# Layer norms of a two-layer decoder step: the first chunk behind a norm input tile by input tile, three tiles centered behind the reciprocal

## The reference

```python
def _layer_norm(x, g, b):
    xf = x.astype(jnp.float32)
    mu = jnp.mean(xf, axis=-1, keepdims=True)
    var = jnp.mean(jnp.square(xf - mu), axis=-1, keepdims=True)
    return ((xf - mu) * lax.rsqrt(var + LN_EPS) * g.astype(jnp.float32) + b.astype(jnp.float32)).astype(x.dtype)
...
        # per sub-layer: x = _layer_norm(DN_ALPHA * x + sublayer(x), g, b)
```

## Time and profile before

| | |
|---|---|
| median of 3 runs | 3062.95 us (3060.9 to 3064.45) |
| the profiled execution, its own time | 3062.5 us |
| its span in the trace | 3060.7 us |
| mean granted TensorE clock | 0.996 |
| busy: PE, DVE, ACT, POOL | 3016.8, 1985.3, 1628.1, 125.0 us |

### The profile page before, as it was taken

The page is one execution under the profiler, slowest core; times in us unless marked ns, Lnnn a source line. Parts: engine busy times, 40 slices in busy tenths (PEclk is TensorE's granted clock), DMA queues, the critical chain, the costliest instruction groups (busy, mean ns, idle before and its releaser), DMA issues.

```text
span 3060.7 us, 60293 instructions
## 1 busy us (share of the span) xinstructions
PE 3016.8 (99%) x25089; PEld 2948.4 (96%) x25089; DVE 1985.3 (65%) x2512; ACT 1628.1 (53%) x1744; POOL 125.0 (4%) x222
## 2 busy tenths in 40 slices
PE   9999999999999999999999999999999999999997
PEld 9999899999999999999999999999999999999997
DVE  5455454677655666667758888777686566556665
ACT  4435575545444445445556767775454444445453
POOL 1010100000000000000000111100000000000000
PEclk9999999999999999999999999999999999999998
DMA  7565667544445445544456776665444544455452
GB/s 273 183 239 205 225 218 278 193 159 167 165 180 199 169 178 205 191 164 179 179 218 216 240 243 230 235 210 194 179 162 179 196 175 172 182 202 182 178 192 84
DMA packets 94523, 598.07 MB, mean 195 GB/s; under 512 B 11120, under 2 KB 11136, under 8 KB 33312
## 3 DMA queue, kind: packets, MB, share of 16 engines
q1 hardware_dynamic: 68688, 498.17, 44.0%
q0 software_dynamic: 25680, 97.69, 9.2%
HBM read 558.66 MB, written 37.15 MB: 195 GB/s over the span
## 4 chain that ended last, share of the span: by engine, by line
PE 92%; DVE 5%; ACT 1%; issue 1%; DMA 1%; DVEq 0%; POOL 0%; POOLq 0%; SPq 0%; ACTq 0%
PE acc L653 29%; PE acc L654 28%; PE acc L655 28%; DVE lo L563 1%; PE aux L2103 1%; PE aux L2426 1%; PE aux L2459 1%; PE aux L2440 1%; DVE x L1789 1%; DVE xl L1802 1%; DVE x L1797 1%; ACT xh L1188 0%; ACT hi L553 0%; PE aux L2188 0%; DMA x<-xsave 0%
## 5 line engine op out<-in xcount | busy, mean ns | idle before, releaser
L653 PE MATMUL acc<-xh,hi 128*128 128x264 f32 x7552 | 2174.8, 288 | 10.0 <-DVE lo L563 5.0
L654 PE MATMUL acc<-xl,hi 128*128 128x264 f32 x7552 | 2146.5, 284 | 0.0
L655 PE MATMUL acc<-xh,lo 128*128 128x264 f32 x7552 | 2139.0, 283 | 0.0
L653 PEld LDWEIGHTS acc<-xh,hi 128*128 128x128 f32 x7552 | 1422.9, 188 | 26.6 <-issue 13.9
L654 PEld LDWEIGHTS acc<-xl,hi 128*128 128x128 f32 x7552 | 1423.1, 188 | 4.2
L655 PEld LDWEIGHTS acc<-xh,lo 128*128 128x128 f32 x7552 | 1419.9, 188 | 0.0
L563 DVE TENSOR_TENSOR lo<-raw,hi 128x2048 fp32r<-128x2048 f32 x473 | 1077.7, 2287 | 381.2 <-ACT hi L553 380.5
L553 ACT ACTIVATE hi<-raw 128x2048 fp32r<-128x2048 f32 x473 | 897.6, 1907 | 492.6 <-DMA raw<-in_w 324.0
L552 ACT ACTIVATE xh<-pj 128x1056 fp32r<-128x1056 f32 x144 | 156.0, 1083 | 340.2 <-PE acc L655 279.6
L560 DVE TENSOR_TENSOR xl<-pj,xh 128x1056 fp32r<-128x1056 f32 x144 | 180.7, 1255 | 203.5 <-ACT hi L553 200.2
L1512 DVE SCALAR_TENSOR_TENSOR stage<-acc,par,stage 128x255 f32<-128x255 f32 x352 | 168.9, 480 | 23.1 <-DVE stage L1512 21.9
(11 more groups left out here) (284 smaller groups left out, 1609.3 us busy)
## 6 DMA issues: line engine op xcount, KB each, us to landing
raw<-in_w SPq DMA_DIRECT2D x473, 1024.0 KB, 4.9
x<-in_ssm POOLq DMA_DIRECT2D x32, 512.0 KB, 4.4
out_ssms<-x POOLq DMA_DIRECT2D x32, 512.0 KB, 5.1
x<-in_ret POOLq DMA_DIRECT2D x16, 512.0 KB, 5.4
out_rets<-x POOLq DMA_DIRECT2D x16, 512.0 KB, 3.9
x<-in_ck POOLq DMA_DIRECT2D x16, 512.0 KB, 3.9
x<-in_cv POOLq DMA_DIRECT2D x16, 512.0 KB, 5.6
pj<-cumd POOLq DMA_DIRECT2D x32, 256.0 KB, 5.7
```

Source lines behind the costliest of these rows:

```text
L653: pe.matmul(out, hi[:, s, w], xh[:, a, :], start=kc == 0 and k == 0, stop=False)
L654: pe.matmul(out, hi[:, s, w], xl[:, a, :], start=False, stop=False)
L655: m = pe.matmul(out, lo[:, r, w], xh[:, a, :], start=False, stop=kc == ph.kc - 1 and k == CK - 1)
```

## The change

In `products` a phase with `split` gets a first chunk of its own (`first_chunk`), with the loop over input tiles outside and that over accumulators inside. It is written out ahead of the loop over iterations, and the rest of the first iteration is written out too. On VectorE only the first tile of group 0 is centered ahead of the reciprocal. The tiles 1, 2 and 3 are centered one by one behind it, between the scalings and the low parts of their neighbours, and each scaling waits for its own centering. Norm 3 keeps `center(0)`. The other lines of the diff count the semaphore `ln_fin` anew, 8 for each norm where it was 5.

```diff
+            def first_chunk():
+
+                s, r = ph.hi(0), ph.raw(0)
+                pe.wait_ge(lo_done, ph.chunk0 + 1)
+                for k in range(CK):
+                    if k < CK - 1:
+                        pe.wait_ge(R["x_first"], (CK - 1) * (split - 1) + k + 1)
+                    else:
+                        pe.wait_ge(R["x_lo"], XB * split + 1)
+                    for n in range(CN):
+                        if k == 0:
+                            pe.wait_ge(drained, 4 * ph.panel0 + n + 1)
+                        w = slice((k * CN + n) * P, (k * CN + n + 1) * P)
+                        out = acc[n][:, 0:T]
+                        pe.matmul(out, hi[:, s, w], xh[:, k, :], start=k == 0, stop=False)
+                        pe.matmul(out, hi[:, s, w], xl[:, k, :], start=False, stop=False)
+                        m = pe.matmul(out, lo[:, r, w], xh[:, k, :], start=False, stop=False)
+                m.then_inc(used, 1)
...
-                            if j == 0 and n == 0 and split:
-                                if k < CK - 1:
-                                    pe.wait_ge(R["x_first"], (CK - 1) * (split - 1) + k + 1)
-                                else:
-                                    pe.wait_ge(R["x_lo"], XB * split + 1)
...
+            elif split:
+                first_chunk()
+                body(Step(0), begun=True)
                 with pe.Fori(0, whole - 1) as r:
                     body(Step(1, r))
...
-                center(0)
+                def center_tile(t):
+                    tt(x[:, t, :], x[:, t, :], lsum[:, :], ALU.add).then_inc(R["ln_fin"], 1)
+
+                if l == 3:
+                    center(0)
+                else:
+                    center_tile(0)
                 dve.wait_ge(R["ln_sqrt"], l + 1)
                 dve.reciprocal(lvar[l], lvar[l]).then_inc(R["ln_fin"], 1)
-                dve.wait_ge(R["ln_fin"], 5 * l + 2)
+                dve.wait_ge(R["ln_fin"], 8 * l + 2)
...
-                for q in range(XB):
+                scale_tile(0)
+                center_tile(1)
+                dve.wait_ge(R["ln_fin"], 8 * l + 3)
+                scale_tile(1)
+                low_tile(0)
+                center_tile(2)
+                low_tile(1)
+                dve.wait_ge(R["ln_fin"], 8 * l + 4)
+                scale_tile(2)
+                center_tile(3)
+                low_tile(2)
+                dve.wait_ge(R["ln_fin"], 8 * l + 5)
+                scale_tile(3)
+                low_tile(3)
+                for q in range(1, XB):
```

More of the change, by code:

```diff
@@ L631, in products, with body @@
         def products(pe, ph, split=None, side=None, front=None, inner=None):
-            def body(i, last=False, front=None):
+            def first_chunk():
[15 more added lines that the diff above has]
+                m.then_inc(used, 1)
+            def body(i, last=False, front=None, begun=False):
                 for j in range(ph.body):
+                    if begun and j == 0:
+                        continue
                     pb, kc = j // ph.kc, j % ph.kc
@@ L638, in body @@
                     s, r = ph.hi(j), ph.raw(j)
-                    if pb == 0 and split is not None and (kc or not split):
+                    if pb == 0 and split is not None and (begun or not split):
                         pe.wait_ge(R["x_lo"], XB * split + kc + 1)
@@ L670, in products @@
                 body(Step(0), False, front)
+                with pe.Fori(0, whole - 1) as r:
+                    body(Step(1, r))
+            elif split:
+                first_chunk()
+                body(Step(0), begun=True)
                 with pe.Fori(0, whole - 1) as r:
@@ L1791, in scaled @@
                 def scaled(q):
-                    dve.wait_ge(R["ln_fin"], 5 * l + (q + 2 if q else 1))
+                    dve.wait_ge(R["ln_fin"], 8 * l + q + 2)
                     v = x[:, group(q), :]
@@ L1817, in norm @@
                     return
-                for q in range(XB):
+                scale_tile(0)
[13 more added lines that the diff above has]
+                for q in range(1, XB):
                     if q == XB - 1:
                         split_lo(dve, lead[l][3][0], Step(0), 3, None)
-                    if q:
-                        center(q)
-                        dve.wait_ge(R["ln_fin"], 5 * l + q + 2)
+                    center(q)
+                    dve.wait_ge(R["ln_fin"], 8 * l + 5 + q)
                     scale_tile(CK * q)
```

## The result

The changed kernel takes 3068.67 us (median of 22 runs, 3064.77 to 3074.11) against 3063.68 us (median of 22, 3059.31 to 3067.14). The ratio is 1.0018 with a 95% interval of 1.0012 to 1.0024: slower, by 5.0 us by the medians and 5.5 us by the ratio. The forecast was 3067.3 us, 3064.4 to 3070.4.

A forecast was written before the change was run, and what follows sets the result against it. VectorE's chain through each norm was taken as the bound: 3062.5 us + 3.15 (1.05 in three norms) + 1.1 or 2.2 for half clock gives 3066.75 or 3067.85, stated as 3067.3; range 3064.4 to 3070.4.

The forecast's parts named there:

- VectorE's chain: In each norm, VectorE's work from first centering to last low part (24.18 us) sets when TensorE's fourth chunk starts.
- a fourth chunk that finds its input there: Sign against the forecast: if TensorE's fourth chunk needn't wait for the last low part, the bound and the sign are wrong.
- Group 1's centering: VectorE's four-tile centering after group 0 would start at 695.53 instead of 694.47, making the last low part 1.05 us later.
- the place of low 2: VectorE, group 0: tile 2's low part no longer fills the time between tile 3's scaling and low part; 0.41 us more exposed.
- A wait of 2.5 us ahead of the second chunk: TensorE would finish the first chunk 1.3 us earlier, then stand about 2.5 us until group 1 is ready.
- half clock behind a norm: TensorE at 1.2 GHz for 3.40 us after its wait, about one time in two; 1.7 us lost, 1.1 reaching the end.
- case A: Likeliest (0.46): VectorE's tail 1.05 us later three times, half clock behind one or two norms; 3067.3 us, 3065.8 to 3068.9.
- C: Slower (0.24): half clock behind all three norms, 3068.95 us, or 3069.4 on the median's footing.
- Case B: Chance 0.19: no half clock behind any norm, only VectorE's 3.15 us, 3065.65 us.
- D: No change (0.06): the one-tile centerings hide wholly in VectorE's waits for `xh`, 3062.5 us.
- E: Faster (0.05): the first chunk's earlier end on TensorE counts, 1.3 us for each of three norms, 3058.6 us.
- The 4.2 us: VectorE's loss over the norms by the skill page's drain rule, about 1.4 us a norm; the prediction kept 1.05 instead.

The follow-up runs named there:

- e1: Kernel before with only TensorE's part of the change (first chunk tile by tile, written out), VectorE in the old order; ratio to before 1.0002, median +2.5 us.
- e2: Kernel before with only VectorE's part of the change (one tile centered ahead of the reciprocal), TensorE in the old order; ratio to before 1.0009, median +3.4 us.
- e4: Changed kernel's TensorE order, VectorE with the old four-tile centering but three scalings first in every group; ratio to the kernel before 0.9984, median -5.1 us.
- e5: Kernel before with three scalings first in every group on VectorE, TensorE exactly as before; ratio to before 0.9983, median -5.8 us.
- e7: Changed kernel with the scaling of tile 3 ahead of the low part of tile 2 in group 0; ratio to the kernel before 1.0011, median +2.8 us.
- e6: Kernel before with only TensorE's first iteration of up0, bc and up1 written out ahead of the loop, all orders as before; ratio 1.0003, median +1.6 us.
- e8: Kernel before without the 12 products of constants in each norm, leaving TensorE idle ahead of the first chunk; ratio to before 0.9996, median -1.9 us.

## Why the prediction was right, point by point

**The bound.** That VectorE's chain sets the norm's length, and not the first chunk's order, was borne out. e1 frees TensorE earlier and gains nothing, e2 lengthens the chain by 1.14 us and loses as much, e4 and e5 shorten it and gain until TensorE itself is the bound. But the chain reaches the last low part only where the clock stays full. In the changed kernel and in e7 it leaves VectorE at the low parts of group 1, and TensorE at half clock is the bound from there. The prediction had named a fourth chunk that finds its input there as a sign that its bound and the sign of the result were wrong. The fourth chunk did find it there, 0.9 us behind the last low part (713.39 to 714.28), and the result has the forecast sign all the same: TensorE was late, VectorE wasn't early. By its own sum, 1.7 us of half clock against 0.60 to spare, a norm with half clock couldn't have a wait there.

**VectorE's steps.** The reciprocal 0.50 us earlier was measured so. The low part of tile 0 came 0.29 us earlier (forecast 0.32). Group 1's centering came 1.13 us later (forecast 1.05); the rest of 0.08 us is spread over handovers. The one-tile centering had been priced at 0.43 us and 0.34 to the next start, and the rows have 0.43 and 0.35 (692.18 to 692.53 in the trace). The prediction put 0.41 us of the loss on the place of low 2, against the order before, and e7, with low 2 moved, gives 0.63 back. (By its own times the forecast delay is 695.53 less 694.47, 1.06.)

**TensorE.** A wait of 2.5 us ahead of the second chunk was forecast and 2.77 came. The near match of 698.2 and 698.15 is in part luck, since norm 0 begins 0.30 us later in this profile and 698.2 was the end of the last issue. Counted from the first centering, the first chunk starts at 4.37 us (forecast 4.39) and ends its issue at 10.27, 0.23 earlier than forecast: of the 0.24 us for a restart only 0.08 show, as a second matmul 0.20 behind the first instead of 0.12. The low parts of group 1 come 0.08 later, which makes up the rest of the longer wait.

**The clock.** The mechanism was right, but the term was mis-sized in both factors, its price too high and its chance too low. The prediction had half clock behind a norm about one time in two. The profile has it behind all three, and by the mean clocks of the 22 runs it came about that often in the runs without a trace too; the two fastest of them, 3064.77 and 3066.08 us, had 0.996, the clock of before. The price was set at 1.1 us each. Measured against e2_dve_only, it is 0.55, 0.72 and 0.72 at the fifth chunk and settles at 0.43, 0.34 and 0.60 at the ninth, 1.4 us in all. The traces show where the estimate went off. The second chunk takes 7.29, 7.34 and 7.46 us in the three norms against 5.93 at full clock, so 1.4 to 1.5 us are lost and not 1.7: half clock begins 0.4 us ahead of the chunk, within the idle time (0.95 in the row of 698.30 to 701.10 puts it at 700.8, the chunk starts at 701.20). The 0.60 us to spare ahead of the fourth chunk are taken up as forecast. Then the fifth chunk comes 5.85 us behind the fourth, not 6.04 (5.92 in norm 1), because the fourth doesn't start behind a wait and the fifth no longer waits for its accumulator. By the ninth another 0.1 to 0.4 us is made up.

**The sum.** The forecast of 3067.3 is 4.8 us above the 3062.5 that it was added to (3067.75 if the 0.45 us to the median are put on it, as the prediction says and case A leaves out). The three norms cost 4.8 us in the traces: 3.4 for VectorE against 3.15, and 1.4 for the clock against 1.1 or 2.2. That the clock's share fits is luck in part: three stretches at 0.46 us each come to the same as one or two at 1.1, and the mechanism was C's, half clock behind all three. The measured 5.0 to 5.5 us hold some tenths more; the stall in `up1` is 0.5 us of the profile, and whether it comes in most runs isn't known. Case B isn't the usual one, though the two fastest runs may be of its kind. D and E are out: no trace shows the centerings hidden, or a fourth chunk freed by the first.

The Trainium skill, page "VectorE: DVE Perf Modes", section "The DRAIN you can't avoid", was quoted in the prediction for the rule that the next instruction doesn't start until the pipe is empty, and the same section goes on: "A next op that is not held starts earlier". The rows agree with that: instructions that wait for nothing still start 0.08 to 0.09 us before the one ahead ends. They don't agree that a semaphore costs nothing extra, since a scaling that waits for the centering ahead starts 0.46 us behind it (690.91 to 691.37) and one instruction that doesn't wait 0.35. The 4.2 us that the prediction worked out by the rule also left out the 0.50 us that the reciprocal gains in each norm; by its own durations that would have been about 0.9 us a norm.

**Open.** The stall of 0.5 to 0.8 us in `up1`, whether the written-out code costs more than the 0.1 to 0.2 us of the traces of e1 and e6 (their medians lie 2.5 and 1.6 us above before, within what the intervals allow for no change), and why half clock follows a given wait in one execution and not in another.

## What to carry to other kernels

Ask which wait ends last in the stage, not which engine waits most often: here the first chunk's new order took away six of the 12 visible waits of TensorE and gained nothing (e1), and one chain on VectorE made up 3.4 of the 4.8 us. When two engines hand tiles back and forth, count how many instructions stand between an operation and the one that needs its partner's answer; moving one instruction was worth 0.6 us of a 24 us chain, and three scalings ahead of the first low part 2.1 us. And an earlier finish that is followed by a longer wait can cost more than it gives, because half clock may follow the wait.

## What the runs showed of the hardware that was not expected

The same wait of TensorE was followed by half clock in one profile and by full clock in another, with the same code there. Over the ten profiles the wait of 2.2 us at about 360 was followed by it in eight, not in before and e1. The wait of 1.8 us at about 1590 was followed by it in five (the changed kernel, e1, e4, e5, e6). All nine longer waits at a norm, 2.77 us in the changed kernel, 2.16 in e7 and 5.6 in e8, three each, were followed by it or had it within them; the three of 1.35 us in e1 weren't. And in e8 the slow clock cost nothing at the end where the engine that it slows had time to spare: the mean granted clock fell from 0.996 to 0.993 and the time didn't rise.
